# Attention on one Trainium2 core: the mask added by TensorE, one minimum and one reciprocal for a pair of heads, and diagonal matrices that turn and norm the probabilities

## The reference, cut to what matters

```python
# first block, per head (dqk = 96), keys = 16 meta tokens and all tokens up to the query
s = einsum('bhqd,bhkd->bhqk', qb, k) * scale
s = where(kpos[None, :] <= qpos[:, None], s, -inf)
o = einsum('bhqk,bhkd->bhqd', softmax(s, axis=-1), v)

# second block, per head (dh = 64) and branch; masked_softmax gives 0 where nothing is seen
def masked_softmax(s, mask):
    s = where(mask, s, NEG_INF)
    return where(mask, softmax(s, axis=-1), 0.0)
# the output is the sum of the three branches, each times its sigmoid gate of (token, head, branch)
```

## Time and profile before

| | us |
|---|---|
| median of 3 runs | 3163.65 |
| range of the runs | 3157.81 to 3178.35 |
| the profiled execution, its own time | 3159.39 |
| its span in the profile | 3158.1 |
| PE busy (share of the span) | 2272.4 (72%) |
| DVE busy | 1802.2 (57%) |
| ACT busy | 426.0 (13%) |
| POOL busy | 1432.2 (45%) |
| mean bandwidth of the DMA | 263 GB/s |

### The profile page before, as it was taken

How to read it: one execution, slowest core, us unless ns; L and a number is a source line. 1 busy time by engine, 2 the same in 40 slices (tenths; PEclk the granted TensorE clock), 3 DMA queues, 4 the chain that set the end, 5 groups by cost and what they waited for, 6 DMA issues and landing times. The chain is left out here.

```text
span 3158.1 us, 24727 instructions
## 1 busy us (share of the span) xinstructions
PE 2272.4 (72%) x8222; PEld 1376.0 (44%) x8222; DVE 1802.2 (57%) x3876; ACT 426.0 (13%) x1209; POOL 1432.2 (45%) x1137
## 2 busy tenths in 40 slices
PE   5997980056673784767674478979957687969989
PEld 3535850023432662322344235758425443437544
DVE  1512119978779677566477897674666854224300
ACT  1212000011200100000000232012000321013310
POOL 0000002377667787778767764676655433100000
PEclk9796995577695796999885557989977688987999
DMA  3310522599889999978889877999998779942376
GB/s 129 121 67 27 173 96 101 157 350 370 282 337 329 333 401 352 321 237 266 293 306 398 288 249 230 394 386 393 363 360 330 259 246 379 340 153 83 126 259 220
DMA packets 291759, 829.57 MB, mean 263 GB/s; under 512 B 23568, under 2 KB 30016, under 8 KB 290864
## 3 DMA queue, kind: packets, MB, share of 16 engines
q0 software_dynamic: 148464, 539.99, 47.7%
q1 hardware_dynamic: 139872, 283.19, 24.7%
q10 hardware_dynamic: 3296, 4.80, 0.4%
HBM read 825.81 MB, written 2.10 MB: 262 GB/s over the span
## 5 line engine op out<-in xcount | busy, mean ns | idle before, releaser
L315 POOL DMA_INDIRECT picks_rows<-peer_u_dram,expert x512 | 723.5, 1413 | 830.2 <-DVE expert L1465 516.2
L315 POOL DMA_INDIRECT picks_rows<-peer_v_dram,expert x512 | 618.1, 1207 | 477.4 <-DVE h L380 354.6
L374 DVE CUSTOM_DVE_ANT_0 picks_rows<-picks_rows,xn 128x1024 f32<-128x1024 f32 x512 | 613.7, 1223 | 169.0 <-DMA picks_rows<-peer_u_dram,expert 144.4
L380 DVE SCALAR_TENSOR_TENSOR h<-picks_rows,picks_weight,h 128x1024 f32<-128x1024 f32 x416 | 535.0, 1286 | 189.4 <-DMA picks_rows<-peer_v_dram,expert 116.3
L465 PE MATMUL psum<-weight_ring,hnT 128*128 128x512 f32 (+4 forms) x576 | 236.9, 573 | 23.0 <-DMA weight_ring<-w_in_dram 10.9
L403 PE MATMUL psum<-picks_rows,picks_diag 128*128 128x512 f32 x384 | 187.3, 625 | 59.9 <-POOL picks_diag L333 59.5
L1753 PE MATMUL psum<-weight_ring,aT 128*128 128x512 f32 x512 | 220.8, 593 | 3.1 <-ACT aT L2060 1.4
L465 PEld LDWEIGHTS psum<-weight_ring,hnT 128*128 128x128 f32 (+1 forms) x576 | 106.2, 187 | 152.4 <-issue 137.5
L874 PE MATMUL psum<-identity_sb,na_probs 128*128 128x128 f32 (+2 forms) x384 | 93.7, 359 | 100.9 <-DVE na_probs L958 79.4
L656 PE MATMUL psum<-identity_sb,n_scaled 128*128 128x128 f32 (+1 forms) x104 | 24.1, 412 | 181.9 <-DVE n_scaled L640 181.9
L1753 PEld LDWEIGHTS psum<-weight_ring,aT 128*128 128x128 f32 x512 | 96.9, 190 | 125.3 <-issue 120.5
(11 more groups left out here) (353 smaller groups left out, 3170.8 us busy)
## 6 DMA issues: line engine op xcount, KB each, us to landing
weight_ring<-w_ff_dram SPq DMA_DIRECT2D x48, 2048.0 KB, 11.0
weight_ring<-w_in_dram SPq DMA_DIRECT2D x44, 2048.0 KB, 13.6
weight_ring<-w_proj_nsa_dram SPq DMA_DIRECT2D x6, 2048.0 KB, 8.1
weight_ring<-w_out_dram SPq DMA_DIRECT2D x6, 2048.0 KB, 14.8
weight_ring<-w_ret_out_dram SPq DMA_DIRECT2D x4, 2048.0 KB, 8.0
weight_ring<-w_mix_out_dram SPq DMA_DIRECT2D x4, 2048.0 KB, 18.9
weight_ring<-w_peer_q_dram SPq DMA_DIRECT2D x4, 2048.0 KB, 13.4
picks_rows<-peer_u_dram,expert POOLq DMA_INDIRECT x512, 7.8
```

The lines of the kernel that those rows point to most:

```text
L315: pool.indirect_dma_start(out=self.rows[:, n % GATHERS, :], out_offset=None, in_=table, in_offset=bass.IndirectOffsetOnAxis(ap=self.expert ...
L374: ins = nc.vector.tensor_tensor_reduce(out=row, in0=row, in1=self.x[t], scale=1.0, scalar=0.0, op0=ALU.mult, op1=ALU.add, accum_out=self.d ...
L380: ins = nc.vector.scalar_tensor_tensor(out=h, in0=row, scalar=self.weight[:, t % 2, k:k + 1], in1=h, op0=ALU.mult, op1=ALU.add)
```

## The change

TensorE adds the mask: behind the score products of both heads of a pair comes, for each head, a product of the identity with the mask into the same PSUM columns. Only the last 128 keys of a causal item are masked (the others always lie before the query), so the mask is cut to 128 columns, and to the compressed keys in that branch. DVE takes the minima of both heads in one reduction that reads PSUM and writes nothing there; so both heads' scores must be there, and both exponentials wait for the same instruction. One reciprocal serves the pair, and one small product brings in the two gates. Where an item has more than 128 keys, the probabilities are no longer scaled: DVE builds for the pair two diagonal matrices (identity times factor, `turner`, 2 x 128 columns), and PE multiplies each 128-key block of unnormed probabilities by the diagonal matrix, a plain product in place of the transpose. Elsewhere (the compressed branch and tile 0 of the second wave) one product scales both heads' probabilities and the transpose stays. The zeroing of unseen compressed keys is gone: the gates of the compressed branch of tile 0 are multiplied once by "anything seen". The semaphores for minima and norms count steps instead of items.

```diff
@@ -162,8 +162,9 @@
 
 
 
-    def __init__(self, q, kT, mask, v, meta, seen, gate, place, ends):
-        self.q, self.kT, self.mask, self.seen, self.gate, self.meta = q, kT, mask, seen, gate, meta
+    def __init__(self, q, kT, mask, v, meta, gate, place, ends):
+        self.q, self.kT, self.mask, self.gate, self.meta = q, kT, mask, gate, meta
         self.set, self.part, self.column = place
         self.start, self.stop = ends
         n = kT.shape[-1]
@@ -171,6 +172,8 @@
         self.blocks = [(P * m, min(P, n - P * m), x) for m, x in enumerate(v)]
         if meta is not None:
             self.blocks.append((n, META, meta[1]))
+        self.by_turn = self.keys > P
 
 
 def linker(eng, signal):
@@ -811,7 +814,8 @@
     g.ended["dve"], g.ended["act"], g.ended["pe"] = s_link.after(0), s_gate.after(0), g.w.end(products[-1][0])
 
 
-def attention_stage(g, tag, items, outputs):
+def attention_stage(g, tag, items, outputs, unseen=()):
 
 
 
@@ -831,10 +835,15 @@
     with ExitStack() as ctx:
         sb = lambda name, shape: ctx.enter_context(nc.sbuf_tensor(f"{tag}_{name}", shape, F32))
         probs, probsT = sb("probs", [P, 4, widest]), sb("probsT", [P, 4, blocks_max * P])
+        turner = sb("turner", [P, 4, P]) if widest > P else None
         least, rowsum, factor = sb("least", [P, 8]), sb("rowsum", [P, 8]), sb("factor", [P, 8])
 
         def pair(s):
             return range(2 * s, 2 * s + 2) if 0 <= s < steps else ()
+        def both(s, slots):
+            return slice(2 * s % slots, 2 * s % slots + 2)
 
         def scores(i):
             keys = items[i].keys
@@ -842,6 +851,12 @@
                 return g.psum[:, 2 * (i % 2):2 * (i % 2) + 2, :].rearrange("p a b -> p (a b)")[:, 0:keys]
             return g.psum[:, i % 4, 0:keys]
 
+        def both_scores(s):
+            keys = items[2 * s].keys
+            if wide:
+                return g.psum[:, 0:4, :].rearrange("p (i a) b -> p i (a b)", i=2)[:, :, 0:keys]
+            return g.psum[:, both(s, 4), 0:keys]
         def turned(i, m, keys):
             if m < 4:
                 return g.psum[0:keys, 4 + i % 2, P * m:P * m + P]
@@ -860,18 +875,27 @@
                     pe.wait_ge(*s_exp.after(i - depth + 1))
                     if wide:
                         pe.wait_ge(*s_copied.after(i - depth + 1))
-                mm = nc.tensor.matmul(scores(i)[:, 0:it.kT.shape[-1]], it.q, it.kT, start=True, stop=True)
+                n = it.kT.shape[-1]
+                nc.tensor.matmul(scores(i)[:, 0:n], it.q, it.kT, start=True, stop=False)
+            for i in pair(s):
+                it = items[i]
+                n, masked = it.kT.shape[-1], it.mask.shape[-1]
+                mm = nc.tensor.matmul(scores(i)[:, n - masked:n], g.identity[:], it.mask, start=False, stop=True)
                 if it.meta is not None:
-                    mm = nc.tensor.matmul(scores(i)[:, it.kT.shape[-1]:it.keys], it.q, it.meta[0], start=True, stop=True)
+                    mm = nc.tensor.matmul(scores(i)[:, n:it.keys], it.q, it.meta[0], start=True, stop=True)
                 mm.then_inc(s_scores.sem, 1)
 
         def turn(pe, s):
             for j in pair(s):
-                pe.wait_ge(*s_normed.after(j + 1))
+                it = items[j]
+                pe.wait_ge(*s_normed.after(s + 1))
                 if j >= 2:
                     pe.wait_ge(*s_copied.after(j - 1))
-                for m, (at, keys, _) in enumerate(items[j].blocks):
-                    mm = nc.tensor.transpose(turned(j, m, keys), probs[:, j % 4, at:at + keys], g.identity[:])
+                for m, (at, keys, _) in enumerate(it.blocks):
+                    if it.by_turn:
+                        mm = nc.tensor.matmul(turned(j, m, keys), probs[:, j % 4, at:at + keys], turner[:, j % 4, :], start=True, stop=True)
+                    else:
+                        mm = nc.tensor.transpose(turned(j, m, keys), probs[:, j % 4, at:at + keys], g.identity[:])
                 mm.then_inc(s_turned.sem, 1)
 
         def value(pe, s):
@@ -901,7 +925,7 @@
 
         def exponentials(act, s):
             for i in pair(s):
-                act.wait_ge(*s_least.after(i + 1))
+                act.wait_ge(*s_least.after(s + 1))
                 if i >= 4:
                     act.wait_ge(*s_turned.after(i - 3))
                 nc.scalar.activation(probs[:, i % 4, 0:items[i].keys], scores(i), ACT.Exp, bias=least[:, i % 8:i % 8 + 1],
@@ -939,32 +963,37 @@
         def vector(dve):
             g.begin(dve)
             link = linker(dve, s_link)
+            for gate, seen in unseen:
+                link(nc.vector.tensor_scalar(gate, gate, seen, None, ALU.mult))
             for s in range(steps):
-                for i in pair(s):
-                    dve.wait_ge(*s_scores.after(i + 1))
-                    nc.vector.tensor_tensor_reduce(out=scores(i), in0=scores(i), in1=items[i].mask, scale=1.0, scalar=-LOWEST,
-                                                   op0=ALU.add, op1=ALU.min, accum_out=least[:, i % 8:i % 8 + 1]).then_inc(s_least.sem, 1)
+                it = items[2 * s]
+                dve.wait_ge(*s_scores.after(2 * s + 2))
+                nc.vector.tensor_reduce(least[:, both(s, 8)], both_scores(s), AX_X, ALU.min).then_inc(s_least.sem, 1)
                 g.picks.use(dve)
-                for i in pair(s):
-                    it, p = items[i], probs[:, i % 4, 0:items[i].keys]
-                    f = factor[:, i % 8:i % 8 + 1]
-                    dve.wait_ge(*s_exp.after(i + 1))
-                    if it.seen is not None:
-                        nc.vector.tensor_tensor(p, p, it.seen, ALU.mult)
-                    link(nc.vector.reciprocal(f, rowsum[:, i % 8:i % 8 + 1]))
-                    if it.gate is None:
-                        ins = nc.vector.tensor_scalar(p, p, f, None, ALU.mult)
-                    else:
-                        ins = nc.vector.tensor_scalar(p, p, f, it.gate, ALU.mult, ALU.mult)
-                    ins.then_inc(s_normed.sem, 1)
+                f = factor[:, both(s, 8)]
+                dve.wait_ge(*s_exp.after(2 * s + 2))
+                link(nc.vector.reciprocal(f, rowsum[:, both(s, 8)]))
+                if it.gate is not None:
+                    link(nc.vector.tensor_tensor(f, f, it.gate, ALU.mult))
+                if it.by_turn:
+                    if s >= 2:
+                        dve.wait_ge(*s_turned.after(2 * s - 2))
+                    ins = nc.vector.tensor_tensor(turner[:, both(s, 4), :], g.identity[:].unsqueeze(1).to_broadcast([P, 2, P]),
+                                                  f.unsqueeze(2).to_broadcast([P, 2, P]), ALU.mult)
+                else:
+                    p = probs[:, both(s, 4), 0:it.keys]
+                    ins = nc.vector.tensor_tensor(p, p, f.unsqueeze(2).to_broadcast([P, 2, it.keys]), ALU.mult)
+                ins.then_inc(s_normed.sem, 1)
                 g.picks.use(dve)
 
         g.w.load_through(nc.sync, None)
         tensor(nc.tensor)
         scalar(nc.scalar)
         vector(nc.vector)
-    for signal in (s_scores, s_least, s_exp, s_normed, s_turned, s_copied, s_values):
+    for signal in (s_scores, s_exp, s_turned, s_copied, s_values):
         signal.count += n_items
+    for signal in (s_least, s_normed):
+        signal.count += steps
     s_out.count += len(outputs)
     g.ended["pe"], g.ended["act"], g.ended["dve"] = s_values.after(0), s_out.after(0), s_normed.after(0)
 
@@ -1882,9 +1911,9 @@
                     for h in range(MH):
                         vh = v[:, :, MV * h:MV * h + MV]
                         items.append(Item(
-                            q=qT[:, h, local(t)], kT=kT[:, h, META:META + keys], mask=tables["mask"][:, S - keys:S + META],
-                            v=[vh[:, m + 1, :] for m in range(t + 1)], meta=(kT[:, h, 0:META], vh[0:META, 0, :]), seen=None,
-                            gate=None, place=(at, h % 2, h // 2), ends=(True, True)))
+                            q=qT[:, h, local(t)], kT=kT[:, h, META:META + keys], mask=tables["mask"][:, S - P:S],
+                            v=[vh[:, m + 1, :] for m in range(t + 1)], meta=(kT[:, h, 0:META], vh[0:META, 0, :]), gate=None,
+                            place=(at, h % 2, h // 2), ends=(True, True)))
                 if items:
                     attention_stage(g, tag(f"ma{which[0]}"), items, [oT[:, :, local(t)] for t in which])
 
@@ -2027,19 +2056,20 @@
                         for branch in range(3):
                             for h in (h0, h0 + 1):
                                 half = slice(HD * (h % 2), HD * (h % 2) + HD)
-                                common = dict(q=qT[half, h // 2, local(t)], gate=branch_gates[:, j, 3 * h + branch:3 * h + branch + 1],
+                                common = dict(q=qT[half, h // 2, local(t)], gate=branch_gates[:, j, 3 * h0 + branch:3 * h0 + branch + 4:3],
```

(10 more changed lines are left out.)

## The result

| | before | after |
|---|---|---|
| median, us | 3171.0 (4 runs) | 3211.63 (4 runs) |
| range, us | 3157.81 to 3181.93 | 3201.76 to 3226.98 |
| ratio after / before | | 1.0149, 95% interval 1.0116 to 1.0182 |
| the profiled execution, own time / span | 3159.39 / 3158.1 | 3213.44 / 3212.1 |

The change costs 1.5% by the ratio on record. The two medians alone, 41 us apart, give 1.3%; the two profiled executions are 54 us apart.

What follows compares the result with a forecast made beforehand. DVE was taken to bound na2_0 and na2_1, PE na2_2 and ma0. Stage terms -2 + 3 + 15 + 4 - 2 + 5 = +23 us gave 3187 against the median of 3163.65; range 3142 to 3232.

Steps and rivals of the forecast that it cites:

- na2_0: Second-wave attention stage of two query tiles: -2 us taken, between -15 (DVE relief) and +12 (PE the bound at half clock).
- ma0: First-wave attention stage, PE-bound at clock 0.54: masks and turns add 0 to +15 us, +4 taken.
- na2_2: Second-wave stage without picks: set of 11.8 us against about 10.3, +15 us taken, bounds +8 and +27.
- the forecast's signs: Signs in na2_2: stage longer by 10 to 20 us, with PE over 0.85 busy.
- The price of a plain product: PE's 128-key blocks: 0.24 us at full clock, so a turned block costs 0.10 more; 0.27 more at half clock.
- that rival: Turned blocks in second-wave stages: a plain product costs four transposes, 86 us less some cover, 3260 us; chance 0.04.
- The DVE term, -15: In na2_0, DVE saves 20 us of work and gets 5 us back as idle time.
- a sign of being wrong: Granted clock in the attention stages moving far from that of before in either direction; no size given.
- that rival's mechanism: In na2_0 and na2_1, DVE relief passes through: -13 or -26 us, time 3138 to 3150; chance 0.2.
- na2_1, ma2 and ma3: One-tile second-wave stage +3 us (-6 to +15); two first-wave stages, -2 and +5 us.
- DVE's relief: DVE work saved: 20 us in na2_0, 14 in na2_1; busy some 30 us less over the three second-wave stages.
- The chain of waits: Exponentials follow one reduction and precede one reciprocal: DVE idles 5 us in na2_0, 8 in na2_1; also in na2_2's set.

Runs made afterwards that it cites:

- before again: The kernel before, unchanged, profiled in a second execution: 3178.65 us.
- e1: Kernel before with TensorE adding the mask and one minimum per pair, normalisation and transposes as before: 3177.51 us, ratio 1.0042.
- e4: Kernel before with TensorE's mask products in addition, DVE still adding the mask with each head's own minimum: 3157.87 us, ratio 0.9968.
- after again: The kernel after, unchanged, profiled in a second execution: 3205.52 us.
- e3: Kernel before with the whole change in stage na2_0 alone: 3154.86 us, ratio 0.9971.
- e7: Kernel before with the change in stage ma0 alone: 3188.0 us, ratio 1.0055.
- e9: Kernel after with a separate minimum for each head, one reciprocal still serving the pair: 3164.35 us, ratio 0.9993 to the kernel before.
- e10: Kernel after with each head's own minimum, reciprocal and scaling: 3176.66 us, ratio 1.0020 to the kernel before.
- e2: Kernel before with one reciprocal per pair and the diagonal matrices, DVE still adding the mask with each head's own minimum: 3165.54 us, ratio 0.9994.
- e8: Kernel before with ma0 using TensorE masks and common minimum, na2_0 the whole change, na2_1 common reciprocal and diagonal matrices: 3135.7 us, ratio 0.9891.
- e5: Kernel before with only waits tied: both exponentials wait for both minima, both norms for both exponentials: 3209.36 us, ratio 1.0115.

## Why the prediction was right, and where it was not

The direction is right, and the size within the range: 3187 was forecast, 3212 measured, between 3142 and 3232. That the sum came so near is in part luck: na2_0 missed by 12 us to one side and ma0 by 19 to the other, and 13 of the 54 us between the profiled executions lie in no attention stage. Part of the miss is the anchor: the median of the first three runs was 3163.65, that of 25 runs in the last comparison 3169.95. The stage terms, forecast against measured (after less before; in brackets after less before again):

| | forecast | measured |
|---|---|---|
| na2_0 | -2 | -13.9 (-12.3) |
| na2_1 | +3 | +4.1 (+4.2) |
| na2_2 | +15 | +18.7 (+17.4) |
| ma0 | +4 | +23.4 (+18.8) |
| ma2 | -2 | -2.0 (-6.7) |
| ma3 | +5 | +7.7 (+3.7) |
| sum | +23 | +38.0 (+25.1) |

**na2_2, right.** The set was put at 11.8 us and took 12.4. The turn of eight blocks is 2.05 us (1.92 forecast), masks 0.66 (0.48), the reduction over 1024 elements 1.23 (1.22), scores and values as said. PE is busy 98.3 of 104 us at a clock of 0.97: the forecast's signs, 10 to 20 us longer and over 0.85 busy. What the sum didn't say is that two limits lie close together: PE's own work, 11.6 us a set, and the tied chain, 12.4. Untying the minimum gains 6.9 us and leaves 11.8 of the 18.7, which is PE's. e1 and e4 alone would have made the tie look like the larger part: 15 less 2.5 of it. While PE still has room, as in e1, the tie costs more.

**The price of a plain product, right.** 0.24 us was taken at full clock and 2.05/8 = 0.256 measured, against 0.14 for a transpose (1.12/8): 1.8 times. (The stretch at full clock in the earlier trace rows has nine records and was divided by eight; the 1.12 us for eight bears the figure out.) The Trainium skill, "TensorE: Matmul & The Clock Gate", section Terms, has transpose mode four times faster for FP32; the trace doesn't agree here, and that rival falls.

**na2_0, mis-sized.** The DVE term, -15, was right in size. Steps in the timeline of DVE, after (start, us, instruction), beside the earlier trace rows:

```profile
1893.48 0.18 DVE L971 TENSOR_REDUCE na_least<-psum 128x2 f32<-128x30 f32 x1
...
1896.55 0.68 DVE L971 TENSOR_REDUCE na_least<-psum 128x2 f32<-128x512 f32 x1
...
1898.35 0.16 DVE L975 RECIPROCAL na_factor<-na_rowsum 128x2 f32<-128x2 f32 x1
1898.54 0.16 DVE L977 TENSOR_TENSOR na_factor<-na_factor,branch_gates 128x2 f32<-128x2 f32 x1
1898.73 0.43 DVE L981 TENSOR_TENSOR na_turner<-identity_sb,na_factor 128x256 f32<-128x256 f32 x1
1899.08 0.68 DVE L971 TENSOR_REDUCE na_least<-psum 128x2 f32<-128x512 f32 x1
```

The compressed step with two picks fell from 3.56 us to 3.07, the 256-key step with one pick from 2.96 to 2.53: 0.49 and 0.43, forecast 0.5 and 0.44. What failed is the step to -2, with PE as the bound at half clock (+12 as the other end). In the first tile PE is busy 76 of 85 us at 0.50, in the second 70.5 of 86, where the clock went up from 0.56 to 0.82, far above what the bound had assumed. The prediction had named a clock far from that of before as a sign of being wrong, and na2_0 under 175 us as half of another. After again has 0.78 there and 177.3 us for the stage. So the relief passed through, and most of that rival's mechanism was true (e3: 0.9971 by this stage alone, na2_0 9 to 10 us shorter). It didn't reach its time because na2_2 and ma0 took more.

**ma0, mis-sized.** +4 was taken of 0 to +15, in the hope that a higher clock gives something back. At the same clock (0.54 before again, 0.55 after) the 72 added records cost 19 us (70.3 or 70.5 less 51.5), with PE busy 66.9 of 70.3 us. The clock is not the kernel's alone: it was 0.60 in the first execution of before (46.9 us) and 0.66 in after again (61.1 us), so between single executions the loss is 10 to 23 us. A higher clock did give something back in after again; in the first execution and in e7 it didn't. The window was also cut at the first output copy, so it showed 33 us of a stage of 47, and the second tile, with twice as many full blocks, was outside it. That PE's work is paid in full here was right.

**na2_1, ma2 and ma3** came as forecast within 5 us, of which an execution moves as much by itself (ma2 63.6 and 68.3 in the same program). In na2_1 the plus is the tie: e9 and e10 bring it to 93.6 and 90.8 us, under the 98.9 of before.

**DVE's relief** was forecast too small: some 30 us less over the second wave's stages, and it is 57 (311.4 to 254.4, by the windows): 40 in na2_0 and na2_1, where the sum had 34, and 17 in na2_2, which it left out. It bought little outside na2_0.

**The chain of waits, underrated.** The working knew of the tie ("both exponentials follow the one reduction") and priced it at 13 us of DVE's idle time in na2_0 and na2_1, besides its place in na2_2's chain. Over the kernel it is dearer: e9 has it back, with 47 us between medians (3211.63 to 3164.35). Between the two profiled executions it is 32 us (3213.44 to 3181.62), of which the six stages hold 25, ma0's 9.8 included. After again has as short an ma0 as e9, and the six stages hold 26 all the same: 12.8 in na2_1, 6.9 in na2_2, 3.8 in na2_0. So na2_1 and na2_2 have 16 to 20 us of it in both executions. The other 15 us of the medians' difference stand in no profile, since e9's profiled execution was 17 us over its median. Which stages hold them stays open.

**Open:** the stretch from ma3 to na2_0 is 889.7 and 891.1 us in the two executions of before and 892.9 to 906.7 in every other kernel, with no code of it changed. In it ACT has, in most of them, waits that neither execution of before shows. The kernel after, then e3 (ACT's waits, 900 to 1810 us; "remote" is a release that the profile ties to no engine of the core):

```profile
ACT nsa_kT_sb L718 <- remote: 15.3, 2, 8.8
```

```profile
ACT pqT L510 <- remote: 16.6, 1, 16.6
```

e3's median is below that of before all the same, so it may belong to the profiled executions only. After again has no such wait and 902.9 us, so these waits are not the whole of it. What it is wasn't found.

## What to carry to other kernels

Merging two heads' instructions saves an engine's time but also ties what waits for them: if the consumers of the first half could have started, price the tie as a wait in the chain. Here merging the reciprocals cost nothing that could be measured (e2, e10), and merging the minima did (e9). Choose the form stage by stage, since one edit made the kernel some 10 us faster in the stage where DVE sets the pace (e3) and 18 us slower in the one where TensorE does (e7). Before a stage's window is read, see that it ends at the last of its output copies.

## What the runs showed of the hardware

- In ma0, where PE is the bound, the granted clock moved the stage's length as much as the whole change did, and it differs between executions: ma0 in one form took 34.5 us at 1.00 and 56.3 at 0.56 (e1, e8). From 80 to 120 us, just before it, the two executions look alike: PE busy 9.25, 10, 10 and 8.5 of 10 us each, at full clock.
- e9's ten runs fall in two groups: six of 3158 to 3165 us with a mean granted clock of 0.835 to 0.838, four of 3180 to 3189 at 0.827 to 0.829. A few runs of such a kernel place its median only to some 10 us. The five runs of the kernel after, 3202 to 3227 at 0.822 to 0.827, are all slower than either group; against the group at 0.827 to 0.829 their first four have a median 29 us higher, where the medians of all runs are 47 apart.
- In na2_2 the granted clock was 0.89 before (PE busy 74 of 86 us), 0.79 with the tie and no added work (e5, 87 of 113), and 0.97 with the added work and each head's own minimum (e9, 95 of 97). In e5 the same 528 records kept PE busy 12.6 us longer than before, so the waits cost more than their own length there. It is not so everywhere: in e8's ma0 the clock was 0.50 from 130 to 170 us with PE busy all the time.
